# Two summed weight tiles rounded one place earlier, in a flow-matching backbone kernel

## What is computed

```python
def _swiglu(h, wg, wu, wd):
    return (jax.nn.silu(h @ wg) * (h @ wu)) @ wd
...
    x = x + 0.5 * g1 * _swiglu(h, p["w_ffn1_gate"], p["w_ffn1_up"], p["w_ffn1_down"])
```

## Time and profile before

| | us |
|---|---|
| median of 3 runs | 2731.36 (2730.28 to 2731.52) |
| the profiled execution, its own time | 2732.1 |
| its span, first to last instruction | 2730.3 |
| TensorE busy with matmuls | 2662.0 (97%) |
| VectorE busy | 2089.2 (77%) |
| ScalarE busy | 1213.6 (44%) |
| GpSimd busy | 625.4 (23%) |

### The profile page before, as it was taken

The page is one execution under the profiler, slowest core; times in us unless marked ns, Lnnn a source line. Parts: engine busy times, 40 slices in busy tenths (PEclk is TensorE's granted clock), DMA queues, the critical chain, the costliest instruction groups (busy, mean ns, idle before and its releaser), DMA issues. The chain is left out here.

```text
span 2730.3 us, 44482 instructions
## 1 busy us (share of the span) xinstructions
PE 2662.0 (97%) x17686; PEld 2524.2 (92%) x17686; DVE 2089.2 (77%) x2832; ACT 1213.6 (44%) x2002; POOL 625.4 (23%) x327
## 2 busy tenths in 40 slices
PE   5999999999999999999999999999999999999997
PEld 3999999987899999999989999999779999999997
DVE  6978879766566788887988878887565668786876
ACT  5523435556422543343564334355563245343433
POOL 1322412023000124232321423300220003232230
PEclk9999999999999999999999999999999999999998
DMA  6434232210243243332234333322113322222312
GB/s 231 159 124 139 93 109 74 70 44 32 74 129 107 100 162 120 124 127 89 89 108 151 112 124 107 95 64 69 29 37 118 129 78 78 93 83 65 108 47 78
DMA packets 87694, 270.90 MB, mean 99 GB/s; under 512 B 8705, under 2 KB 12545, under 8 KB 87361
## 3 DMA queue, kind: packets, MB, share of 16 engines
q1 hardware_dynamic: 86048, 263.51, 29.3%
q10 hardware_dynamic: 1440, 4.56, 0.5%
HBM read 265.12 MB, written 2.92 MB: 98 GB/s over the span
## 5 line engine op out<-in xcount | busy, mean ns | idle before, releaser
L695 POOL TENSOR_TENSOR sums_raw<-raw_pairs 128x1024 f32<-128x1024 f32 x88 | 243.8, 2770 | 1613.7 <-DVE weights_lo L1830 1029.3
L731 PE MATMUL ps<-h_hi,weights_hi 128*128 128x322 f32 (+1 forms) x1408 | 440.3, 313 | 8.6 <-DVE t_lo L1830 3.1
L735 PE MATMUL ps<-h_hi,weights_lo 128*128 128x322 f32 (+1 forms) x1408 | 437.2, 311 | 0.0
L733 PE MATMUL ps<-h_lo,weights_hi 128*128 128x322 f32 (+1 forms) x1408 | 436.7, 310 | 0.0
L1830 DVE TENSOR_TENSOR weights_lo<-sums_raw,weights_hi 128x1024 fp32r<-128x1024 f32 (+2 forms) x296 | 329.5, 1114 | 65.2 <-ACT weights_hi L1341 28.2
L731 PE MATMUL ps<-t_hi,weights_hi 128*128 128x322 f32 (+1 forms) x1056 | 332.3, 315 | 5.3 <-DVE h_lo L1830 5.3
L735 PE MATMUL ps<-t_hi,weights_lo 128*128 128x322 f32 (+1 forms) x1056 | 327.5, 310 | 0.0
L733 PE MATMUL ps<-t_lo,weights_hi 128*128 128x322 f32 (+1 forms) x1056 | 326.5, 309 | 0.0
L731 PE MATMUL ps<-a_hi,weights_hi 128*128 128x320 f32 x1408 | 322.1, 309 | 3.6 <-DVE tmp L2032 3.3
L733 PE MATMUL ps<-a_lo,weights_hi 128*128 128x320 f32 x1408 | 320.8, 308 | 0.0
L735 PE MATMUL ps<-a_hi,weights_lo 128*128 128x320 f32 x1408 | 320.6, 309 | 0.0
(11 more groups left out here) (288 smaller groups left out, 5741.6 us busy)
## 6 DMA issues: line engine op xcount, KB each, us to landing
raw_pairs<-in_w_up SPq DMA_DIRECT2D x87, 1024.0 KB, 5.0
wm<-in_w_mod SPq DMA_DIRECT2D x72, 512.0 KB, 3.8
raw<-in_w_merge SPq DMA_DIRECT2D x32, 704.0 KB, 4.1
sums_raw<-in_w_down SPq DMA_DIRECT2D x56, 384.0 KB, 3.2
sums_raw<-in_w_down SPq DMA_DIRECT2D x64, 320.0 KB, 2.9
wm<-in_w_mod SPq DMA_DIRECT2D x48, 256.0 KB, 2.9
raw<-in_w_in SPq DMA_DIRECT2D x16, 512.0 KB, 3.6
late_wm<-in_w_mod SPq DMA_DIRECT2D x16, 512.0 KB, 3.6
```

Source lines behind the costliest of these rows:

```text
L695: nc.gpsimd.tensor_tensor(sums_raw[:, UNIT:3 * UNIT].rearrange("p (s c) -> p s c", s=2), w.rearrange("p (s c) -> p s c", s=2)[:, :, 0:UNIT ...
L731: nc.tensor.matmul(out, whi, v, start=first, stop=False)
L733: nc.tensor.matmul(out, whi, v, start=False, stop=False)
L735: mm = nc.tensor.matmul(out, wlo, v, start=False, stop=last)
```

## The change

On ScalarE the rounding `hi_34` of a pair moves from its own cycle (behind `hi_11` of the next pair, ahead of `silu_of`) to the end of the cycle before, ahead of that cycle's `up_bias`. On VectorE `lo_34` moves the same way: from behind `gate_scaled` and `lo_11` to the end of the cycle before, behind `lo_22`, which is ahead of `c12` and `gate_scaled`. Of 88 pairs 72 are not the first of a chunk, and these are moved. The waits inside `hi_34` and `lo_34` stay.

```diff
@@ ScalarE, cycle(g, c, n)
                     if following:
                         hi_11(g + 1)
                     if not first:
-                        hi_34(g)
                         silu_of(g - 1)
...
                     else:
                         hi_22(g + 1)
+                        hi_34(g + 1)
                     up_bias(g)
@@ VectorE, cycle(g, c, n)
                     if following:
                         lo_11(g + 1)
                     if not first:
-                        lo_34(g)
                         gated(g - 1)
...
                     else:
                         lo_22(g + 1)
+                        lo_34(g + 1)
```

## The result

The changed kernel takes 2846.27 us (median of 4 runs, 2845.08 to 2848.32) against 2731.44 for the kernel before on the same chip: ratio 1.0422, 95% interval [1.0409, 1.0435]. It is 114.8 us slower; 2843 was forecast. The profiled execution has a span of 2845.6 us.

A forecast was written before the change was run, and what follows sets the result against it. TensorE was 97% busy and VectorE had next to no room; extra port blocking would make VectorE the bound. Chunk losses 25.8 + 16.9 + 13.5 + 30.4 + 19.0 + 7 = 112.6, taken as 112 us, gave 2843 us; range 2780 to 2868.

The forecast's parts named there:

- VectorE as full as TensorE, the cycle 12.83 us: VectorE from one `lo_34` to the next: 12.83 us without idle time, 10.78 its own and 2.05 blocking.
- Who is there first keeps the ports, and they take turns: VectorE instructions with two SBUF inputs and GpSimd's adds exclude each other; a large add holds 2.26 us, a small 1.15.
- Rival 1: VectorE keeps the ports when its next instruction is ready: cycle 13.8 us, total 2789; chance 0.15.
- Rival 2: Faster or unchanged: `gate_scaled` and neighbours pass GpSimd unhindered, or sums start no earlier; 2728 us; chance 0.08.
- Rival 3: The loss feeds on itself: late TensorE delays `c12` or `hi_34`, half a us per cycle, 2870 us; chance 0.05.
- Blocked 1.93 + 1.10 + 1.05: GpSimd's adds block `gate_scaled`, `lo_11` and `gated` on VectorE: 4.08 us instead of 2.05, cycle 14.86 us.
- The chain to the down tiles: From P3(0)'s end to the down tiles: 70.4 us for six pairs against 61.8 before with two conditioning tiles.
- the forecast's n-2: Cycles with GpSimd sums beside them in a chunk of n pairs, 14.86 us each; first two pairs' sums fall among down tiles.
- `a_rest`'s share: In the down tiles of eight chunks of five, the last pair's `a_rest` comes late: 0.85 x 8 = 7 us.
- ScalarE's wait at nothing: On ScalarE, `hi_34` waits for P3, so `up_bias` comes about 1 us later; cost nothing, as ScalarE is half idle.
- `c21` late for the first down tile, `a_rest` for chunks of five: TensorE's waits at the down tiles: some 20 us for `c21`, and 7 us lost to `a_rest`.

The follow-up runs named there:

- the last experiment: The kernel before, with GpSimd's large add made as two adds of 128x512: 2730.18 us, ratio 0.9999.
- the short add: The changed kernel with GpSimd's large add on an eighth of its columns, except for each step's first pair: 2746.87 us, ratio 1.0054.
- the split: The changed kernel with GpSimd's large add made as two halves, one plane each: 2788.38 us, ratio 1.0210.

## Why the forecast was right

*VectorE as full as TensorE, the cycle 12.83 us.* It held: what was put on VectorE's cycle was paid for (in VectorE's half of the change alone, 16.68 us a cycle gave 248 us). A little room there is all the same: the cycle of 12.99 us in the last experiment cost nothing.

*Who is there first keeps the ports, and they take turns.* Shown in the changed kernel's rows, and by the short add and the split, in which nothing but the length or number of GpSimd's adds was changed. Rival 1, in which VectorE keeps the ports between ready instructions, falls with `lo_11`'s 1.75 us. Rival 2, in which `gate_scaled` passes unhindered, falls with line 2048's median of 2.60 us. Rival 3, in which the loss feeds on itself, falls with the cycle shown: between its instructions VectorE has no idle time of more than 0.13 us, so nothing came late in turn.

*Blocked 1.93 + 1.10 + 1.05.* Measured 2.74 - 0.83 = 1.91, 1.75 - 0.68 = 1.07 and 1.90 - 0.82 = 1.08. The cycle was 14.61 us (333.28 - 318.67) instead of 14.86: the steps between instructions at the end, `lo_s` to `c21` and `lo_22` to `lo_34`, are 1.13 and 0.60 us where I had 1.24 and 0.70.

*The chain to the down tiles.* The third chunk's down tiles began at

```profile
372.24 0.54 PE L731 MATMUL ps<-a_hi,weights_hi 128*128 128x320 f32 x2 [1.85 <-DVE tmp L2032]
```

with P3 of its first pair at 300.89, so 71.35 us behind it against 63.59 before: 7.8 more, where 8.6 was forecast. In the profiled executions, over all 16 chunks, the parts compare like this:

| | forecast, us | measured, us |
|---|---|---|
| cycles, from `c21` of a chunk's first pair to its first down tile | 105.6 | 99.9 |
| down tiles, from the first matmul to the last | 7 | 12.6 |
| all else | 0 | 2.8 |

The mechanism was right, but that the sum came within 4 us is in part luck: three terms were mis-sized by -5.7, +5.6 and +2.8 us. The cycles came out short mainly because each beside GpSimd is 0.25 us shorter than forecast. Against that, the second step's last chunk has a fifth cycle beside GpSimd, which the forecast's n-2 left out (its down tiles lie in another buffer, so the next step's first sums are not held back): five large adds start between 1328 and 1387 us, and its cycles got 10.5 us longer instead of the 7.9 that the forecast's working gives. The down tiles lost more than `a_rest`'s share in the eight chunks of five (5.9 in all, forecast 7; from its own rows the forecast should have had 8.45 - 0.55 - 7.1 = 0.80 a chunk, 6.4): in four chunks of six they lost 1.6 to 1.8 us each, and the granted clock is low at the start of all four, see below. The 2.8 us of all else are not attributed.

*ScalarE's wait at nothing.* Nearly so: 5 us when alone. What it costs inside the changed kernel no run separates.

*`c21` late for the first down tile, `a_rest` for chunks of five.* 16 waits of 23.4 us and 8 of 4.0. I had named 80 us for weight rests and 20 for `c21`; the first was 56.1. TensorE's busy time, which I expected unchanged, rose by 38.5 us; the last section says how much of it the clock can be.

## What to carry over

Before an instruction moves, look at what it releases on another engine and what will then stand beside it. Here the moved instruction did the same work in the same time and, but for the first cycle of a chunk, waited for nothing. But it moved ahead of 2.0 us of VectorE's work, and so released three adds on GpSimd in front of three instructions that need the same ports, where two adds from PSUM had stood. A duration with two values in one trace (0.69 and 1.87 us for the same tile shape) is the sign to look for, and an engine that takes turns with another has to be read by which instruction stands behind the start of the other's.

## What was not expected

TensorE's granted clock. Its mean fell from 0.994 to 0.985. In the low stretches it is 0.5, so they add up to 2 x 0.015 x 2845.6 = 85 us, against 2 x 0.006 x 2730.3 = 33 us before. One of the new stretches stands right behind a wait of TensorE for `c21` (first chunk, 1.80 us idle up to 135.25). Columns: the stretch, its length, busy us and instructions of each engine, the granted clock, the DMA share, GB/s:

```profile
131.50:136.10 4.60, 2.80 (x20) 2.57 (x19) 4.47 (x9) 1.85 (x3) 0.00 (x0) 1.00 0.19 44
136.10:139.50 3.40, 3.40 (x15) 3.40 (x15) 1.91 (x3) 2.21 (x5) 0.00 (x0) 0.51 0.63 212
139.50:143.00 3.50, 3.50 (x25) 3.50 (x25) 2.20 (x3) 1.13 (x2) 0.00 (x0) 0.99 0.26 81
```

For 3.4 us TensorE ran at about 1.2 GHz, 15 matmuls where 25 fit at 2.4, and the down tiles, which TensorE bounds, lost 1.6 us. Behind waits of 1.80, 1.87, 1.87 and 5.41 us for `c21` the down tiles met such a stretch, behind waits of 1.85 (the third chunk), 1.79 and 1.88 they did not. So a wait of this length sometimes goes with the lower clock and sometimes does not. Where VectorE is the bound such a stretch costs less: of eight among the cycles, three are followed by a cycle that is 0.4 to 0.7 us longer (15.29, 15.27 and 15.00 us from `c21` to `c21`, 14.62 in the others), five by none.

The clock accounts for at most 26 us of TensorE's time here (half of 85 - 33), of which the four down phases make some 6.6, and so not for all of the 38.5 us by which TensorE's busy time rose. A part of the rest can be how the profile counts: a matmul is shown with 0.31 us while the next starts 0.15 later, so each wait adds 0.16 us of busy time that would otherwise be overlap. By this estimate some 70 waits more add 11 us. What decides whether the clock falls was not tried.
